# A two-layer encoder on one core: matrix terms of light experts and of the merged branches interleaved with adds and transposes

## The reference

```
h = rms_norm(x);  proj = h @ w_in                      # u_hyena | q | k | v | gates
y_h = hyena_mixer(...);  y_a = diff_attention(...)
merged = gates[0] * (y_h @ w_hy_o) + gates[1] * (y_a @ w_at_o)
x = x + merged @ w_out
layer 0:  x = x + (silu(h @ w_gate) * (h @ w_up)) @ w_down            # dense, width 2752
layer 1:  the same with 8 experts of width 2752, each token through the top 2 of its router
```

## Time and profile before

| | |
|---|---|
| median of 3 runs | 1399.92 us |
| the profiled execution | 1401.25 us |
| its span, first to last instruction | 1399.4 us |
| mean granted TensorE clock | 0.989 |
| TensorE matrix multiplies busy | 1323.0 us, 95% |
| VectorE busy | 1143.3 us, 82% |
| ScalarE busy | 881.6 us, 63% |
| read from HBM | 375.83 MB, 281 GB/s over the span |

### The profile page before, as it was taken

One profiled execution on the slowest core, in us unless ns is written; L12 is line 12 of the kernel. 1 busy time (PEld: TensorE's weight loads), 2 busy tenths in 40 slices (PEclk: granted clock), 3 DMA queues, 4 the chain that ended last, 5 costly groups with the idle time before them and its releaser, 6 DMA issues.

```text
span 1399.4 us, 17878 instructions
## 1 busy us (share of the span) xinstructions
PE 1323.0 (95%) x6156; PEld 992.3 (71%) x6156; DVE 1143.3 (82%) x1233; ACT 881.6 (63%) x965; POOL 64.0 (5%) x64
## 2 busy tenths in 40 slices
PE   6999989999999999899999998989989999898998
PEld 3887767888887887578666676666766667666666
DVE  5988777644447889875998988989879998899898
ACT  4445644534435345634767778987779877798775
POOL 0011010100000110000030000000000000000200
PEclk9999999999999999999999999999999999999999
DMA  7443333965474334133999998999989999899996
GB/s 284 181 159 143 121 107 125 379 271 187 173 294 180 136 135 166 75 113 122 366 342 373 416 370 347 421 362 423 377 338 422 371 415 382 345 419 365 414 401 242
DMA packets 63443, 394.01 MB, mean 282 GB/s; under 512 B 7186, under 2 KB 7758, under 8 KB 23450
## 3 DMA queue, kind: packets, MB, share of 16 engines
q1 hardware_dynamic: 58666, 374.85, 69.0%
q10 hardware_dynamic: 2848, 11.53, 2.0%
q0 software_dynamic: 1872, 6.91, 1.4%
HBM read 375.83 MB, written 17.43 MB: 281 GB/s over the span
## 4 chain that ended last, share of the span: by engine, by line
PE 64%; DVE 21%; issue 6%; DMA 5%; ACT 4%; DVEq 0%; POOL 0%; SPq 0%; ACTq 0%
PE bank L1672 14%; PE bank L1673 14%; DVE w_lo L1111 14%; PE bank L1947 11%; PE bank L1924 7%; PE bank L1719 5%; DMA raw<-in_moe 5%; ACT w_hi L727 3%; PE bank L1714 2%; PE bank L1825 1%; PE bank L1685 1%; DVE ys L1100 1%; PE bank L1818 1%; PE bank L1934 1%; DVE tmp L1100 1%
## 5 line engine op out<-in xcount | busy, mean ns | idle before, releaser
L1111 DVE TENSOR_TENSOR w_lo<-raw,w_hi 128x2048 fp32r<-128x2048 f32 (+2 forms) x383 | 794.1, 2089 | 110.4 <-ACT w_hi L727 108.0
L727 ACT ACTIVATE w_hi<-raw 128x2048 fp32r<-128x2048 f32 (+2 forms) x383 | 670.4, 1756 | 156.3 <-PE bank L1947 54.0
L1672 PE MATMUL bank<-w_hi,hT_hi 128*128 128x512 f32 (+3 forms) x968 | 384.9, 398 | 0.9 <-issue 0.7
L1673 PE MATMUL bank<-w_hi,hT_lo 128*128 128x512 f32 (+3 forms) x968 | 376.7, 389 | 0.0
L1672 PEld LDWEIGHTS bank<-w_hi,hT_hi 128*128 128x128 f32 (+1 forms) x968 | 171.3, 177 | 50.7 <-issue 3.7
L1673 PEld LDWEIGHTS bank<-w_hi,hT_lo 128*128 128x128 f32 (+1 forms) x968 | 171.4, 177 | 45.1 <-issue 1.0
L1924 PE MATMUL bank<-w_lo,hT_hi 128*96 128x512 f32 (+3 forms) x616 | 162.1, 387 | 0.9 <-DVE w_lo L1111 0.9
L1924 PEld LDWEIGHTS bank<-w_lo,hT_hi 128*96 128x96 f32 (+1 forms) x616 | 103.5, 169 | 37.1 <-DVE w_lo L1111 3.5
L2007 PE MATMUL bank<-w_lo,hT_hi 128*128 128x512 f32 (+1 forms) x264 | 78.1, 414 | 11.1 <-DVE w_lo L1111 10.8
L1719 PE MATMUL bank<-w_lo,hT_hi 128*128 128x512 f32 x352 | 87.0, 389 | 0.0
L1947 PE MATMUL bank<-w_hi,act_lo 128*96 128x512 f32 (+1 forms) x294 | 79.0, 394 | 5.5 <-DVE act_lo L1449 5.5
(11 more groups left out here) (279 smaller groups left out, 1346.4 us busy)
## 6 DMA issues: line engine op xcount, KB each, us to landing
raw<-in_moe SPq DMA_DIRECT2D x224, 1024.0 KB, 9.3
raw<-in_mix SPq DMA_DIRECT2D x56, 1024.0 KB, 5.1
raw<-in_dense SPq DMA_DIRECT2D x28, 1024.0 KB, 5.0
raw<-in_moe SPq DMA_DIRECT2D x43, 512.0 KB, 4.4
raw<-in_moe SPq DMA_DIRECT2D x16, 768.0 KB, 10.5
slot_h<-x_squared ACTq DMA_DIRECT2D x1, 5632.0 KB, 40.9
slot_y<-x_squared ACTq DMA_DIRECT2D x1, 5632.0 KB, 16.7
raw<-in_dense SPq DMA_DIRECT2D x5, 512.0 KB, 3.2
```

The lines of the kernel that those rows point to most:

```text
L727: nc.scalar.activation(HI[:, split_slot, 0:width], RAW[:, raw_slot, 0:width], ACT.Copy)\
L1111: vec.tensor_tensor(LO[:, split_slot, 0:width], RAW[:, raw_slot, 0:width], HI[:, split_slot, 0:width].bitcast(F32), ALU.subtract).then_inc ...
L1672: mm(out_, left[0], right[0], start=start, stop=False)
L1673: mm(out_, left[1], right[1], start=False, stop=False)
```

## The change

Four edits go together.

1. Step mT is cut into mTa and mTb, each with two banks and eight transposes (`turn_merged`). TensorE does mTa between the hi and the lo terms of pa1, after merged has reached 2, and mTb between the hi and the lo terms of the first slab of wo0, after merged has reached 4. n1 of layer 0 is issued right behind mTb. ScalarE and VectorE take the parts of mTa before they turn to what follows pa1: on VectorE the subtraction for mTa now stands ahead of pa1's multiplications and additions. wo0's first slab waits for mTa's banks alone and its second for mTb's.
2. At the start of a light block add_lo goes between slab 4's hi and lo terms, and the transpose of the activation between slab 5's.
3. At its end the tokens' transposes move behind the transpose of the last activation, and add_lo goes between slab 33's hi and lo terms.
4. ScalarE's and VectorE's lists at the end of a light block follow: the tokens' parts come behind the last activation's parts, and VectorE multiplies before it splits slab 34 and subtracts the activation before it splits slab 35.

No instruction is added or taken away; in all three groups the same ones run in another order, save that n1's and mT's loops are written elsewhere.

```diff
@@ -122,10 +122,10 @@
         ("aT2", [2]), ("sc3", [6, 7]), ("av2", [3]), ("ci1", [4, 5]), ("aT3", [2]), ("yT", [0, 1]),
-        ("av3", [3]), ("ph0", [4, 5]), ("yaT", [6, 7]), ("ph1", [0, 1]), ("pa0", [2, 3]), ("pa1", [4, 5]),
-        ("mT", [6, 7, 0, 1]), ("wo0", [2, 3]), ("wo1", [4, 5]), ("fht", [6, 7, 2, 3])]
+        ("av3", [3]), ("ph0", [4, 5]), ("yaT", [6, 7]), ("ph1", [0, 1]), ("pa0", [2, 3]), ("mTa", [6, 7]), ("pa1", [4, 5]),
+        ("mTb", [0, 1]), ("wo0", [2, 3]), ("wo1", [4, 5]), ("fht", [6, 7, 2, 3])]
 PLAN_MOE = [("rt", [0, 1]), ("pos", [1])]
-NEXT_HIDDEN = {"mT": ("n1", [4]), "wo1": ("n2", [6])}
+NEXT_HIDDEN = {"wo0": ("n1", [4]), "wo1": ("n2", [6])}
@@ -778,6 +778,8 @@
                     ahead(step)
+                elif step == "mTa":
+                    ahead("pa1")
                 if step == "ht":
@@ -847,10 +849,10 @@
                              *((event("o_ss", layer), h + 1) if tb == 1 else (None, None)))
-                elif step in ("yT", "yaT", "mT", "fht"):
+                elif step in ("yT", "yaT", "mTa", "mTb", "fht"):
                     if step == "fht":
                         break
-                    at = 4 if step == "yaT" else 0
+                    at = 4 if step in ("yaT", "mTb") else 0
                     for i in range(len(BANKS[step])):
@@ -1005,9 +1007,9 @@
                 silu_light(qb + NCH, k0 + NCH, 0, TAIL)
-                turned_tokens_hi(b + 1, CAP)
                 ffn_split(35, n0, r0, D // 2)
                 turned_hi_light(qb + NCH)
+                turned_tokens_hi(b + 1, CAP)
                 ffn_split(FFN_SLABS, n0, r0, 4 * CHUNK)
@@ -1245,6 +1247,8 @@
                     split_to(first + LAST_SLAB[step] + 2, stage)
+                elif step == "mTa":
+                    split_to(first + LAST_SLAB["pa1"] + 2, stage)
                 if step[:2] == "hf":
@@ -1362,8 +1366,8 @@
                             ALU.mult, ALU.mult, *(drain_of(layer, step, 0) if tb else (None, None)))
-                elif step in ("yT", "yaT", "mT"):
-                    at = 4 if step == "yaT" else 0
+                elif step in ("yT", "yaT", "mTa", "mTb"):
+                    at = 4 if step in ("yaT", "mTb") else 0
                     for i in range(len(BANKS[step])):
@@ -1552,11 +1556,11 @@
                 chunk(28, qb + NCH - 1, 1, n0, 8 * TAIL)
+                mult_light(qb + NCH, 0, TAIL)
                 ffn_split(34, n0, D)
-                mult_light(qb + NCH, 0, TAIL)
+                turned_lo_light(qb + NCH)
+                ffn_split(35, n0, D // 2)
                 turned_tokens_lo(b + 1, CAP)
-                ffn_split(35, n0, D // 2)
-                turned_lo_light(qb + NCH)
                 ffn_split(FFN_SLABS, n0, 4 * CHUNK)
@@ -1687,14 +1691,15 @@
-        def project(layer, step, n, k0, nk, start, stop, turned_w, turned_by=None):
+        def project(layer, step, n, k0, nk, start, stop, turned_w, turned_by=None, amid=None):
...
                 if turned_by and kd % 2 == 0:
-                    wait_drained(pe, layer, turned_by, kd // 2)
+                    by = turned_by[kd // 4] if len(turned_by) == 2 else turned_by[0]
+                    wait_drained(pe, layer, by, kd // 2 % len(BANKS[by]))
                 if turned_w:
@@ -1704,6 +1709,8 @@
                         hi_terms(bank(step, tb)[:, :], (HTH[:, kd, tok], HTL[:, kd, tok]), (w_hi, w_hi), start and k == 0)
+            if amid:
+                amid()
             pe.wait_ge(lo_ready, n + 1)
@@ -1719,6 +1726,21 @@
+        def turn_merged(layer, step):
+
+            half = ("mTa", "mTb").index(step)
+            pe.wait_ge(event("merged", layer), 2 + 2 * half)
+            for i in range(2):
+                bank_free(layer, step, i)
+                for j in range(4):
+                    kd, tb = 4 * half + 2 * i + j // 2, j % 2
+                    ins = turn(bank(step, i)[:, j * P:(j + 1) * P], GATES[:, tb, 0, kd * P:(kd + 1) * P])
+                fill(layer, step, i, ins)
+            if step == "mTb" and layer + 1 < DEPTH:
+                pe.wait_ge(event("hidden_loaded", layer + 1), 4 * 16)
+                bank_free(layer, "n1", 0)
+                fill(layer, "n1", 0, mm(bank("n1", 0)[0:FH, 0:T], R["wf1"][:, :], R["zT"][:, :], start=True, stop=True))
+
         def hold_clock(n):
@@ -1741,7 +1763,7 @@
             for step, banks in plan(layer):
-                if step in ("fht", "rt", "pos"):
+                if step in ("mTa", "mTb", "n1", "fht", "rt", "pos"):
                     continue
@@ -1751,18 +1773,20 @@
                     if step[:2] in ("ph", "pa"):
-                        project(layer, step, last, 4 * (step[:2] == "pa"), 4, True, True, False)
+                        project(layer, step, last, 4 * (step[:2] == "pa"), 4, True, True, False, None,
+                                (lambda: turn_merged(layer, "mTa")) if step == "pa1" else None)
                     else:
...
                             project(layer, step, last - 1 + part, 4 * part, 4, part == 0, part == 1,
-                                    step in ("v", "x1", "x2"), {"v": "ht", "wo0": "mT"}.get(step))
+                                    step in ("v", "x1", "x2"), {"v": ("ht",), "wo0": ("mTa", "mTb")}.get(step),
+                                    (lambda: turn_merged(layer, "mTb")) if step == "wo0" and part == 0 else None)
                             if step == "wo1" and part == 0:
...
                 own = layer + (step[0] == "n")
-                if step in ("f1", "n1"):
+                if step == "f1":
                     pe.wait_ge(event("hidden_loaded", own), 4 * 16)
@@ -1806,10 +1830,8 @@
                     bank_free(layer, step, i)
-                    if step == "mT":
-                        pe.wait_ge(event("merged", layer), 2 + i // 2 * 2)
                     dst = bank(step, i)
-                    if step in ("f1", "n1"):
+                    if step == "f1":
                         ins = mm(dst[0:FH, 0:T], R["wf1"][:, :], R["zT"][:, :], start=True, stop=True)
@@ -1828,14 +1850,11 @@
                         ins = mm(dst[:, :], DFT[:, 1, 1, i, :], im, start=False, stop=True)
-                    elif step in ("ht", "mT"):
+                    elif step == "ht":
                         for j in range(4):
...
                             col, to = slice(kd * P, (kd + 1) * P), dst[:, j * P:(j + 1) * P]
-                            if step == "mT":
-                                ins = turn(to, GATES[:, tb, 0, col])
-                            else:
-                                ins = mm(to, X[:, tb, col], DIAG[:, tb, :], start=True, stop=True)
+                            ins = mm(to, X[:, tb, col], DIAG[:, tb, :], start=True, stop=True)
                     elif step in ("vT", "x1T", "x2T"):
@@ -1995,12 +2014,14 @@
-            def gate_up_light(n, s, k0, nk, width, parity):
+            def gate_up_light(n, s, k0, nk, width, parity, amid=None):
...
                     mm(PS[parity][:, 0:2 * width], HTH[:, k0 + k, 0:2 * LCAP], w_hi, start=k0 + k == 0, stop=False)
+                if amid:
+                    amid()
                 pe.wait_ge(lo_ready, n + 1)
@@ -2021,7 +2042,7 @@
-            def down_light(n, s, q, start, tiles=(0, 1)):
+            def down_light(n, s, q, start, tiles=(0, 1), amid=None):
@@ -2068,14 +2091,11 @@
                         opening = start and j == 0
-                        gate_up_light(n0 + p, slot(p), 0, 4, CHUNK, 1 - j)
+                        gate_up_light(n0 + p, slot(p), 0, 4, CHUNK, 1 - j, (lambda: add_lo(k0, 0)) if opening else None)
+                        if not opening:
+                            turn_act_light(q - 1)
+                        gate_up_light(n0 + p + 1, slot(p + 1), 4, 4, CHUNK, 1 - j, (lambda: turn_act_light(q - 1)) if opening else None)
                         if opening:
-                            add_lo(k0, 0)
-                        else:
-                            turn_act_light(q - 1)
-                        gate_up_light(n0 + p + 1, slot(p + 1), 4, 4, CHUNK, 1 - j)
-                        if opening:
-                            turn_act_light(q - 1)
                             pe.wait_ge(y_taken, 2 * b + 2)
@@ -2092,10 +2112,9 @@
                 gate_up_light(n0 + 32, slot(32), 4, 4, TAIL, 0)
+                down_light(n0 + 33, slot(33), q, False, amid=lambda: add_lo(k0 + NCH, 0, TAIL))
+                turn_act_light(q + 1)
                 turn_tokens(TOK_HEAVY, tok_heavy_loaded, l + 2)
-                add_lo(k0 + NCH, 0, TAIL)
-                down_light(n0 + 33, slot(33), q, False)
-                turn_act_light(q + 1)
                 down_light(n0 + 34, slot(34), q + 1, False, tiles=(0,))
```

## The result

The changed kernel takes 1391.63 us (median of 7 runs, 1389.01 to 1394.18); the kernel before, run beside it, 1400.73 us (7 runs, 1398.13 to 1405.73). The ratio is 0.9935, 95% interval 0.9924 to 0.9946: 9.1 us less. 1390.2 had been forecast, within 1386.0 to 1396.0. The profiled execution of the changed kernel took 1394.18 us, the longest of its seven, with a span of 1392.4.

A forecast was written before the change was run, and what follows sets the result against it. TensorE, busy 95%, was taken as the bound, with transfers bounding light blocks' middles and engine chains their ends. Terms 2.4 + 1.7 + 3.2 + 1.5 + 0.9 = 9.7 us off the 1399.92 median gave 1390.2 us, range 1386.0 to 1396.0.

The forecast's parts named there:

- Merged branches: Between pa1's and wo0's terms: split transposes shorten TensorE's gap, 2.4 us in layer 1 and 1.7 us in layer 0.
- thin cover of 0.3 us: Layer 1's merged branches: the second half of transposes finds its sums ready 0.3 us before TensorE reaches it.
- Rival (c): Merged branches: second half waits for sums its first half's low parts push back; 1394.3 us, chance 0.07.
- Ends: End of each light block: TensorE goes on 1.07 us sooner, 3.2 us in all; bounds 0.5 and 1.2 per block.
- Clock at the ends: End of block 1: the fall to 1.2 GHz after the wait goes, 1.5 us; bounds 0 and 1.5.
- Starts: Start of each light block: earlier silu, mostly lost to slabs not landed; 0.1, 0.4 and 0.4, 0.9 us in all.
- the 0.42 us: Light blocks: last wait comes 82.69 us into block 2 against 82.27 in block 1; used to size the gain at starts.
- upper bound of 4.9 us: Starts of light blocks: the engines' gains counted in full, 0.5 + 2.2 + 2.2 us.
- (a): Starts of light blocks count in full, because slabs asked for earlier land earlier: 13.7 us gained, 1386.2 us, chance 0.16.
- (b): Light-block ends partly given back through late VectorE, clock falls as before, less at layer 0 and starts: 1394.7 us, chance 0.23.
- (d): Light-block ends: one wait becomes two, six more clock falls of 1.5 us make it slower, 1400.7 us; chance 0.04.
- What would show it wrong: TensorE waiting for VectorE in heavy blocks' first slabs, lower clock at more ends, or light blocks over 2 us shorter each.

The follow-up runs named there:

- no_ends: The changed kernel with the order at the ends of the light blocks put back as before: 1393.55 us, ratio 0.9944 to the kernel before.
- after_dve: The changed kernel with only VectorE's order at light-block ends altered, slab 34 split ahead of the multiply: 1390.34 us, ratio 0.9937 to the kernel before.
- before_hold: The kernel before with unread multiplies in TensorE's waits, ten at the start and six at the end of each light block: 1396.07 us, ratio 0.9966.
- after_seam: The changed kernel loading half of slabs 4 and 5 in the three heavy blocks after light ones: 1386.8 us, ratio 0.99 to the kernel before.

## Why the prediction came out

The time was right to 1.4 us, and in part by luck. By the means above, the 9.1 us gained are about 6.0 at the mixers, where 4.1 had been forecast, and about 3 in the blocks, where 5.6 had been; the two errors cancel. Within the blocks the light ones gained more than forecast and the heavy ones gave back what the forecast had them carry on.

- **Merged branches**, 2.4 and 1.7 us: measured 2.44 and 1.68 against the profiled execution of before (by the prediction's own figures two groups of 0.82 us leave 2.5 and not 2.4 of 4.13 us; the lo terms behind a group take 0.1 longer). The mechanism held, and so did the thin cover of 0.3 us. Layer 0 kept its lead through the feed-forward part: the changed kernel stood 3.1 us ahead at 231 us and 3.2 at 570. Rival (c) is out. The term left out is the clock: 1.6 us in layer 1 in five of six executions and in layer 0 in two of six, which the one execution read did not show.
- **Ends**, 1.07 us each: measured 1.2 (8.86 us from slab 32 to the end became 7.65), with 0.21 us of waiting left of 1.53, where 0.5 had been allowed. The step that failed is its last sentence, that "the heavy block starts at full pace and carries the gain on". It looked at VectorE's splits and the tokens, and these came in time; it did not follow the raw slot that slab 34 holds, though its own times (slab 34 split until 1112.8, the next block at 1115.1) put its release 2.3 us before the seam instead of 4.1, and slab 4 was late. The ends alone are worth 1.7 us.
- **Clock at the ends**, 1.5 us: right in size (1.49 us of the first seam, none left in the changed kernel), but one execution was read as if the fall belonged to block 1. By the profiles of all kernels the clock was lowered at 7 of 18 ends in the old order without fill (once in before, three times in `no_ends`), at none of 18 in a new order (`after_dve`'s among them), and at none of 6 filled ones. 3 ends x 7/18 x 1.5 us make 1.8 us in the mean.
- **Starts**, 0.9 us: measured 0.0, 1.2 and 1.7 up to slab 32, 2.9 in all. "Whoever gets through the start sooner meets slabs that have not landed" held for what the engines gain at equal clock: the first two silus come 1.3 and 0.8 us earlier (7.15 and 15.02 us into each block), and nothing of it is left at slab 32. The step that failed is the comparison behind the 0.42 us, that block 2 makes up most of what the clock costs it because it ends little later than block 1. Block 1 takes 1.2 us longer than the others at the same clock (75.2 against 74.0 in `before_hold`; why is not shown), and the fall costs block 2 its 1.6 us in full. The clock was lowered at 12 of 15 starts in the old order, at 5 of 18 in the new, at none of 3 whose one long wait was filled and at none of 6 in the new order with the last of the three waits filled. The upper bound of 4.9 us, set aside, is passed only with short slabs, 5.7.
- **Rivals.** (a), 1386.2, would have the starts kept in full because slabs land earlier; at equal clock they were not. `after_seam` came to 1386.8, but with six loads halved. The transfers ran at 425 to 428 GB/s at the starts, where 420 had been read for the middle. (b) had part of the ends given back in the heavy block, by VectorE's lateness and a clock that still falls; the giving back came, from slabs, and the clock held. (d) went the other way: more, shorter waits let the clock fall less often.
- **What would show it wrong** named light blocks shorter by over 2 us each: two of the three were. By its own test the account of the starts was wrong. What it named as right came too: 0.21 us of wait at the ends, no gap between pa1's and wo0's terms, and 3.1 us of ScalarE waiting for slabs in the middle of the first light block instead of 2.1.

Left open: why the first light block is slower than the other two at the same clock, and how the 3 us left for the blocks divide; one profile each shows 1.2. The clock also falls where no edit reaches: from 585 us on the kernel before had a granted clock of 0.75 for 13.8 us in its profiled execution and the changed kernel 1.00 in the same steps, which makes 1.9 us of the difference of the two traces; and between 641 and 696 us the changed kernel had 0.91 where before had 0.97, which takes 2.7 us off it again.

## What to carry to other kernels

When an end or a start is tightened, ask when the last buffers before the seam come free relative to the first large load after it, not only when the engines are ready; shortening two loads there is a cheap test of it. A ring counted in slots holds little where small pieces fill it, here 2.75 MB in six slots. In this kernel a wait of 0.9 to 2.6 us on TensorE cost up to 1.6 us more than its length, by the clock, in some executions and not in others, so a wait read from one execution may be priced too low; multiplies that nobody reads, put into the wait, show how much of a reordering's gain was only that. Filling the waits of the light blocks brought 4.7 us to the kernel before; reordering them about 3, by difference (9.1 less the mixers' 6.0).

## What the runs showed that was not expected

The same wait in the same code is followed by the lower clock in one light block and not in the next: 12 of 15 starts with 2.45 to 2.65 us idle before the down terms, 7 of 18 ends with about 1.5 us, 5 of 18 starts where the waits are some 0.9, 0.8 and 1.24 us, 5 of 6 times beside the 2.27 us of layer 1's merged branches. Ten multiplies in 2.35 us were enough to hold it at the starts, six at the ends. Transfers at the start of light blocks reached 428 GB/s with one core running. The Trainium skill (DMA: Bandwidth & Descriptors, Where 436 GB/s comes from) lets HBM bind near 358; for one core running alone these rows go against that.
